# The first stick-breaking pair's chain ahead of two weight splits, and one score pair a quarter slot later

## What is computed

```python
h = x
m = dsa_stick_mixer(h, even_w_in, kv_norm, w_uk, w_uv, even_w_out)
h = layer_norm(ALPHA * h + m); h = layer_norm(ALPHA * h + swiglu(h))
m = moba_mixer(h, odd_w_in, odd_w_out)
h = layer_norm(ALPHA * h + m); h = layer_norm(ALPHA * h + swiglu(h))

# stick-breaking, per head, strictly causal (s < t)
z = q @ k.T * HEAD_DIM ** -0.5
log_1m = where(strict, log_sigmoid(-z), 0)
log_rem = reverse_cumsum(log_1m) - log_1m
a = where(strict, exp(log_sigmoid(z) + log_rem), 0)
out = a @ v
# DSA, per head: softmax over the 64 keys that an indexer picks per query, with ALiBi
```

## Time and profile before

| | |
|---|---|
| median of 3 runs | 618.19 us (618.13 to 618.28) |
| profiled execution | 618.07 us |
| its span, first to last instruction | 616.3 us |
| TensorE busy | 603.6 us, 98% |
| VectorE busy | 412.9 us, 67% |
| ScalarE busy | 339.6 us, 55% |
| GpSimd busy | 25.9 us, 4% |
| DMA | 109.48 MB, mean 178 GB/s |

### The profile page before, as it was taken

One profiled execution on the slowest core, in us unless ns is written; L12 is line 12 of the kernel. 1 busy time (PEld: TensorE's weight loads), 2 busy tenths in 40 slices (PEclk: granted clock), 3 DMA queues, 4 the chain that ended last, 5 costly groups with the idle time before them and its releaser, 6 DMA issues.

```text
span 616.3 us, 10303 instructions
## 1 busy us (share of the span) xinstructions
PE 603.6 (98%) x3729; PEld 527.5 (86%) x3729; DVE 412.9 (67%) x668; ACT 339.6 (55%) x631; POOL 25.9 (4%) x49
## 2 busy tenths in 40 slices
PE   7999999999999999999999999999999999999995
PEld 6988887798888888888899999878988888888884
DVE  4698746677756655665886676667776556666546
ACT  5776767265654554455556666653655544555430
POOL 0102012020000000000020000002000000000000
PEclk9999999999999999999999999999999999999999
DMA  8876434446755565555438434451775665556401
GB/s 270 271 237 242 137 103 135 173 148 223 244 176 185 186 204 187 183 187 192 138 115 278 162 130 138 136 209 66 263 231 191 204 203 183 184 181 202 137 1 68
DMA packets 31203, 109.48 MB, mean 178 GB/s; under 512 B 3440, under 2 KB 4464, under 8 KB 31040
## 3 DMA queue, kind: packets, MB, share of 16 engines
q1 hardware_dynamic: 29600, 102.77, 50.2%
q0 software_dynamic: 1568, 6.23, 2.9%
HBM read 107.94 MB, written 1.05 MB: 177 GB/s over the span
## 4 chain that ended last, share of the span: by engine, by line
PE 91%; DMA 3%; DVE 2%; ACT 2%; SPq 1%; issue 1%; DVEq 0%; POOL 0%
PE bank L976 27%; PE bank L892 24%; PE bank L954 12%; PE bank L895 12%; DMA raw<-stream_in 3%; PE bank L906 3%; PE bank L933 2%; PE bank L885 2%; PE bank L1025 2%; PE bank L1036 1%; PE bank L1016 1%; DVE wlo L605 1%; PE bank L939 1%; PE bank L1223 1%; ACT whi L334 1%
## 5 line engine op out<-in xcount | busy, mean ns | idle before, releaser
L605 DVE TENSOR_TENSOR wlo<-raw,whi 128x1024 fp32r<-128x1024 f32 x190 | 226.5, 1221 | 68.1 <-ACT whi L334 67.9
L334 ACT CAST whi<-raw 128x1024 fp32r<-128x1024 f32 x190 | 192.5, 1049 | 22.7 <-DMA raw<-stream_in 22.4
L892 PE MATMUL bank<-hTs,whi 128*128 128x512 f32 x640 | 160.1, 392 | 0.0
L892 PEld LDWEIGHTS bank<-hTs,whi 128*128 128x128 f32 x640 | 116.1, 189 | 21.4
L976 PE MATMUL bank<-whi,oThi 128*128 128x512 f32 x240 | 94.9, 395 | 0.0
L976 PE MATMUL bank<-whi,oTlo 128*128 128x512 f32 x240 | 93.7, 390 | 0.0
L976 PE MATMUL bank<-wlo,oThi 128*128 128x512 f32 x240 | 93.5, 390 | 0.0
L895 PEld LDWEIGHTS bank<-hTs,wlo 128*128 128x128 f32 x640 | 87.3, 190 | 6.3
L895 PE MATMUL bank<-hTs,wlo 128*128 128x256 f32 x640 | 89.2, 282 | 0.0
L954 PE MATMUL bank<-hTs,whi 128*128 128x256 f32 x320 | 60.6, 289 | 0.0
L976 PEld LDWEIGHTS bank<-whi,oThi 128*128 128x128 f32 x240 | 45.1, 188 | 10.0 <-issue 1.5
(11 more groups left out here) (153 smaller groups left out, 701.5 us busy)
## 6 DMA issues: line engine op xcount, KB each, us to landing
raw<-stream_in SPq DMA_DIRECT2D x190, 512.0 KB, 4.5
qT<-ln_rows_in POOLq DMA_DIRECT2D x8, 512.0 KB, 5.1
v<-xT_in SPq DMA_DIRECT2D x4, 256.0 KB, 4.8
kT<-stream_in SPq DMA_DIRECT2D x4, 256.0 KB, 5.0
h<-x_in POOLq DMA_DIRECT2D x1, 1024.0 KB, 7.2
out<-h SPq DMA_DIRECT2D x4, 256.0 KB, 2.0
dist<-consts_in POOLq DMA_DIRECT2D x1, 384.0 KB, 3.6
ukv<-w_uk_in POOLq DMA_DIRECT2D x1, 256.0 KB, 5.6
```

The lines of the kernel that those rows point to most:

```text
L334: nc.scalar.copy(whi[:, c % RING, j * HW:(j + 1) * HW], raw[:, c % RAW, j * HW:(j + 1) * HW]).then_inc(whi_ready, 1)
L605: nc.vector.tensor_tensor(wlo[:, c % RING, cols], raw[:, c % RAW, cols], whi[:, c % RING, cols].bitcast(F32), ALU.subtract).then_inc(wlo_r ...
L892: mm(dst[:], whi[:, slot, off + k * P:off + (k + 1) * P], hTs[:, k].rearrange("p j s -> p (j s)"), start=(k == 0), stop=False)
```

## The change

Three edits. On ScalarE and VectorE, the splits of chunks 6 and 7 leave the straight-line code and stand in slot 0 behind the chain of stick pair 0; the split of chunk 8's first half follows them on both engines (on VectorE it stood ahead of the chain). On TensorE, a new constant `S_LATE` = 10 puts the first quarter of slot 10 ahead of the scores of DSA pair 2 instead of behind them, and VectorE splits the half of slot 10 ahead of that pair's logits. No instruction is added or taken away.

```diff
--- before.py
+++ after.py
@@ -177,7 +177,7 @@
         FILL0 = [(4 + s // 2, s % 2) for s in range(12)] + [(10, 0), (11, 0), (10, 1), (11, 1), (12, 0), (12, 1)]
         Z_AT, R_AT, BV_AT = {0: 0, 3: 1, 8: 2, 11: 3}, {2: 0, 5: 1, 10: 2, 13: 3}, {4: 0, 7: 1, 12: 2, 15: 3}
         S_AT, T_AT, AV_AT = {5: 0, 7: 1, 10: 2, 12: 3}, {7: 0, 9: 1, 12: 2, 14: 3}, {8: 0, 10: 1, 13: 2, 15: 3}
-        Z_LATE = 8
+        Z_LATE, S_LATE = 8, 10
 
 
         SLOTS1 = 22
@@ -439,13 +439,11 @@
             split_hi(5)
             act.wait_ge(ctr_done, 1)
             nc.scalar.copy(cT, bank[7][:, S:2 * S]).then_inc(cT_ready, 1)
-            split_hi(6)
             evac_proj(3, 3, kT[:, 0:2, :])
             act.wait_ge(kA_done, 1)
             for j in range(2):
                 nc.scalar.copy(kT[:, 4 + 2 * j:6 + 2 * j, :], bank[6 + j][:].rearrange("p (k s) -> p k s", k=2)
                                ).then_inc(kA_ready, 1)
-            split_hi(7)
 
 
             def evac_l0(c):
@@ -484,6 +482,9 @@
                         nc.scalar.activation(e, e, ACT.Exp, scale=-1.0).then_inc(e_ready, 1)
                         act.wait_ge(e_ready, n + 1)
                         nc.scalar.activation(e, e, ACT.Ln, bias=1.0).then_inc(l_ready, 1)
+                if s == 0:
+                    split_hi(6)
+                    split_hi(7)
                 if s != Z_LATE:
                     fill_split_hi(8 + s // 2, s % 2)
                 if s in T_AT:
@@ -742,12 +743,10 @@
             split_lo(5)
             topk_round(1)
             topk_round(2)
-            split_lo(6)
             topk_round(3)
             dve.wait_ge(vA_done, 1)
             for t in range(2):
                 nc.vector.tensor_copy(v[:, t, 512:1024], bank[2 + t][:]).then_inc(vA_ready, 1)
-            split_lo(7)
             topk_round(4)
 
 
@@ -762,10 +761,13 @@
             for s in range(SLOTS0):
                 if s - 1 in S_AT:
                     normalise(S_AT[s - 1])
+                if s == S_LATE:
+                    split_lo_half(8 + s // 2, s % 2)
                 if s in S_AT:
                     for n in (2 * S_AT[s], 2 * S_AT[s] + 1):
                         logits(n, 2.0 ** (-8.0 * (n + 1) / A_HEADS), dsel[:])
-                split_lo_half(8 + s // 2, s % 2)
+                if s and s != S_LATE:
+                    split_lo_half(8 + s // 2, s % 2)
                 if s in Z_AT:
                     for n in (2 * Z_AT[s], 2 * Z_AT[s] + 1):
                         dve.wait_ge(l_ready, n + 1)
@@ -774,6 +776,10 @@
                         nc.vector.scalar_tensor_tensor(out=scratch[:, 2 + n % 2, :], in0=bank[n % 2][:, 0:TRI],
                                                        scalar=0.0, in1=scratch[:, n % 2, :], op0=ALU.max, op1=ALU.add
                                                        ).then_inc(sp_ready, 1)
+                if s == 0:
+                    split_lo(6)
+                    split_lo(7)
+                    split_lo_half(8, 0)
                 if s < 3:
                     topk_round(5 + s)
                 if s == 3:
@@ -1191,6 +1197,8 @@
                     transpose_probs(2 * T_AT[s])
                 if s in Z_AT and s != Z_LATE:
                     stick_scores(Z_AT[s])
+                if s == S_LATE:
+                    fill_l0(*FILL0[s], 0)
                 if s in S_AT:
                     j = S_AT[s]
                     pe.wait_ge(proj_evac, 9 if j >= 2 else 6)
@@ -1200,7 +1208,8 @@
                     else:
                         pe.wait_ge(logits_done, 2 * j)
                     score_pair(j, 4 + j, 4 + j)
-                fill_l0(*FILL0[s], 0)
+                if s != S_LATE:
+                    fill_l0(*FILL0[s], 0)
                 if s in T_AT:
                     transpose_probs(2 * T_AT[s] + 1)
                 if s == Z_LATE:
```

## The result

| | before | changed |
|---|---|---|
| median | 618.16 us (618.01 to 618.28, 4 runs) | 625.53 us (623.95 to 626.44, 4 runs) |
| ratio | | 1.0114, 95% interval 1.0099 to 1.0129 |
| profiled execution | 618.07 us | 623.95 us |
| its span | 616.3 us | 622.2 us |
| its mean granted clock | 0.998 | 0.992 |

The change is slower by 7.4 us, where I forecast 3.9 and gave a range up to 625.2. The profiled execution is the fastest of the four.

The account below looks back on a forecast made before the run. TensorE was taken to bound the kernel, with 91% of the chain that ended last. A 5.3 us stall less gains of 0.26, 0.68 and 0.48 gave +3.9 on 618.07: 622.0 us, range 619.4 to 625.2.

Parts of the forecast that it names:

- part 3: Scores of stick pair 1: chunk 9's late first half delays pair 0's exponentials on ScalarE; TensorE stalls 5.3 us.
- Part 1: Before the first stick scores: the two splits leave the path, kT is copied earlier; gain 0.26 us.
- Part 2: At `stick_rest`: pair 0's chain runs first, so the mask is there before TensorE comes; gain 0.68 us.
- Part 4: Slot 10: chunk 9 products cover the 0.69 us wait for q's copy, VectorE's order gives some back; gain 0.48 us.
- The clock: Behind the stall at pair 1: TensorE's clock drops to half, costing 2.4 us more, 624.4 us; chance 0.35.
- 2 (in time): Slot 2: chunk 9 lands in time, no stall, only the gaps are won, 616.7 us; chance 0.05.
- 3 (short stall): Scores of pair 1: chunk 9's half lands in under 3.9 us, stall 2.5 us, 619.2 us; chance 0.08.
- 4 (a waiting tail): Slots 5 to 9: late splits of chunks 9 to 11 make TensorE wait another 1 to 3 us, 624; chance 0.04.

Follow-up runs that it names:

- the last experiment: Decoupled kernel with VectorE's logits of DSA pair 2 again ahead of the split of chunk 13's first half in slot 10: 616.81 us, ratio 0.9975.
- x later: Changed kernel with the load of x moved behind the masks of stick pair 1: 624.65 us, ratio 1.0095.
- the split alone: Changed kernel without its slot 10 part (`S_LATE` set to 99), so the moved splits only: 624.97 us, ratio 1.0099.
- early exponentials: Changed kernel with pair 0's two exponentials on ScalarE directly behind the splits of chunks 6 and 7 in slot 0: 621.17 us, ratio 1.0035.
- decoupled kernel: Changed kernel with pair 0's exponentials early, chunk 9's casts behind pair 1's chain and q copy, top-k rounds 5 to 7 ahead of chunk 8's split: 617.45 us.
- early exponentials and x later: Changed kernel with pair 0's exponentials ahead of the casts of chunks 8 and 9, and x loaded behind stick pair 1's masks: 618.38 us, ratio 1.0002.

## Why the prediction was wrong, point by point

*Direction and the mechanism of the stall* held: the wait sits where part 3 put it, behind the exponentials that follow chunk 9's first half on ScalarE; taking them out of that row took the wait away. The clock's part did not hold. Step by step, with the profiled execution:

- **Part 1**, kT earlier, 0.26. The scores of pair 0 began at 39.11, not at 38.77. This execution was already 0.24 behind the one of before when TensorE began the first split chunk (15.36 against 15.12 in the timelines), so the part brought 0.16.
- **Part 2**, 0.68: right. The mask was there before TensorE came at 47.25. TensorE reached pair 1 at 50.60 (forecast 50.46). (The prediction names the two old waits in one order and gives their times in the other: 48.02 is that of `stick_rest`, 82.28 that of `score_pair`.)
- **Part 3**, the stall, 5.3: 5.48. The chain's end (43.07 for 42.72), the issue (47.65 for 47.27), the landing (53.95 for 53.7) and the release (56.08 for 55.75) all came within 0.4. The reason given for the slow landing was not borne out: I took x for the cause, and with x gone the half took 6.5 us. So it is partly luck that 6.4 fitted; the row of 6.9 that I leaned on had x and only one other half in front, not two. The Trainium skill (DMA: Bandwidth & Descriptors, "Anatomy of one DMA") gives its 2.0 us plus the bytes at 436 GB/s for a transfer that GpSimd issues, and only x is one; the estimate that I made from it had a stall of 3.6, and here the measurement decides. In the slices from 47 to 55 the DMA engines moved between 242 and 434 GB/s.
- **Part 4**, 0.48: 0.39 (0.69 gone, 0.30 new instead of the 0.21 worked out). The expected give-back through VectorE's order is shown by the last experiment, where it is gone.
- **The clock** is the step that failed. I priced it at 2.4, as a rival with a chance of 0.35, and put the forecast on the case without it, though the only row I had, a fall 4.0 us after the last product, spoke for a fall in a stall of 5.3. In the three profiled executions of the changed kernel it fell each time and cost 1.55, 2.5 and 2.0 us; it fell in the two other traces with this wait too (x later, and the split alone). "A stall a microsecond shorter escapes" was wrong as well: in the experiment with early exponentials the clock fell behind an idle time of 2.6 us and cost 1.4, while one of 1.44 us, with x later besides, cost none. The Trainium skill (TensorE: Matmul & The Clock Gate, "Why this matters for your kernels") warns of such gaps, and these traces agree.

With the clock the forecast would have read 624.4, and medians of 625.53, 624.93 and 624.48 were measured. The profiled execution of the first adds up: 5.48 + 1.55 + 0.24 - 0.16 - 0.68 - 0.39 = +6.0, with a span 5.9 longer. The three other executions of that group were 1.3 to 2.5 us longer still. Other traces show a clock loss 1 us larger, a half that lands up to 1.6 us later (but only where TensorE was kept running), and a second fall at 14 us that cost 1.5. Which of them it was here was not profiled and stays open. The range ended at 625.2, a landing of 7.2 and a clock price fixed at 2.4; a second fall, or anything else that the stall does not cause, had no room in it.

Of the rivals, 2 (in time), 3 (short stall) and 4 (a waiting tail) did not occur: slots 5 to 9 show no new wait in the changed kernel. The tail came up only in the experiment that removed the first wait.

## What to carry to other kernels

When a weight split is moved behind other work, follow its buffer: the load that reuses it goes out later by the same time, and everything that stands behind that load's first user on an in-order engine is late with it. Place short steps that TensorE waits for ahead of a cast that waits for DMA, not behind it; here the cast could be late without harm. Price a TensorE stall of some microseconds with the clock included: here it added 1.5 to 2.5 us to one of 5.5. And read the clock over the whole span before an execution's length is put down to one stall: one profile here had lost 1.5 us near the start, away from the change.

## What the runs showed of the hardware

- When the clock falls varies. It fell about 2 us after TensorE's last product in the changed kernel's first profile, 3.4 in that of the third chip (0.54 in the slice 53 to 54, with TensorE idle from 49.7), 4.0 at the end of the kernel before. With early exponentials TensorE had resumed at 61.91 after 2.6 us of idle, and the clock fell in the slice 62 to 63, under the resumed work. 24 products of zeros kept it at 1.00 through a wait of 7.1 us, of which the last 1.45 were idle.
- Two GpSimd masks took 4.07 us instead of 0.87 when three of VectorE's two-input subtractions ran without a break; nearly all of it was the second mask, which ended 0.27 us after the third subtraction. The Trainium skill (GPSIMD Engine Reference, "Specifications") says that its SBUF interfaces are shared with VectorE and contended when a VectorE instruction has two SBUF inputs; the trace agrees.
- With the halves of chunk 8 in front of it, the first half of chunk 9 took 6.1 to 6.6 us in most traces and 7.6 to 7.9 in four. In those four TensorE kept running, and a packet of the instruction queue was moved 2.0 to 2.2 us before the half landed; in the traces of the changed kernel TensorE stood still, and the first such packet came at 55.9 to 56.6, behind the landing. In the decoupled kernel the packet came 0.1 us before the first half landed, and it was the next half that took 8.1; with early exponentials and x later it came 0.4 us before, and neither half was that late. That the instruction load makes the difference was not tried.
